# One tile buffer goes from V's gather ring to U's in a mixer and expert-lookup layer

## What is computed

```python
q = (xt @ w_query).reshape(T, Hh, 2, PEER_HALF)              # 8 heads
s = jnp.einsum('thpc,pnc->thpn', q, sub_keys)
sv, si = lax.top_k(s, K)                                     # K = 16
...
fv, fi = lax.top_k(cand, K)
eidx = jnp.take_along_axis(cidx, fi, axis=-1)                # 16 of 16384 experts per head
g = jax.nn.softmax(fv, axis=-1)
ue = expert_u[eidx]
ve = expert_v[eidx]
act = jax.nn.gelu(jnp.einsum('td,thkd->thk', xt, ue))
return jnp.einsum('thk,thkd->td', g * act, ve)
```

## Time and profile before

| | |
|---|---|
| median of three runs | 3078.46 us |
| profiled execution | 3075.11 us |
| its span, first to last instruction | 3073.6 us |
| TensorE busy (matmul) | 2595.0 us, 84% |
| VectorE busy | 2138.0 us, 70% |
| POOL busy | 1633.1 us, 53% |
| ScalarE busy | 804.2 us, 26% |
| bytes moved | 1071.89 MB, 349 GB/s over the span |
| of that by POOL's gathers | 805.40 MB |

### The profile page before, as it was taken

How to read it: one execution, slowest core, us unless ns; L and a number is a source line. 1 busy time by engine, 2 the same in 40 slices (tenths; PEclk the granted TensorE clock), 3 DMA queues, 4 the chain that set the end, 5 groups by cost and what they waited for, 6 DMA issues and landing times.

```text
span 3073.6 us, 38707 instructions
## 1 busy us (share of the span) xinstructions
PE 2595.0 (84%) x13398; PEld 1675.4 (55%) x13398; DVE 2138.0 (70%) x5237; ACT 804.2 (26%) x1798; POOL 1633.1 (53%) x1565
## 2 busy tenths in 40 slices
PE   8999998766867768688777686667999999999998
PEld 6898544334444434454444452445666666666664
DVE  5451666569899788888898786773677755555556
ACT  2231113113223233232342333881111101000001
POOL 0000477677666656666656566673544554555554
PEclk9999999878878889898888797788999999999999
DMA  7103799999999999999999899999999999999998
GB/s 263 49 29 141 259 371 382 388 399 367 398 392 361 401 346 379 394 349 359 381 360 365 315 368 380 372 384 399 372 359 367 378 403 401 397 401 401 403 402 316
DMA packets 340953, 1071.89 MB, mean 349 GB/s; under 512 B 33876, under 2 KB 74136, under 8 KB 339736
## 3 DMA queue, kind: packets, MB, share of 16 engines
q0 software_dynamic: 221184, 805.40, 67.7%
q1 hardware_dynamic: 119576, 264.01, 23.1%
HBM read 1029.03 MB, written 40.26 MB: 348 GB/s over the span
## 4 chain that ended last, share of the span: by engine, by line
PE 58%; DVE 14%; DMA 12%; ACT 5%; issue 5%; POOL 4%; SPq 1%; DVEq 0%; ACTq 0%; POOLq 0%
PE bank L2220 21%; PE xs_ahead L2220 16%; PE xs L2220 15%; PE acc L2220 6%; DMA weights<-u_blocks 5%; DVE work L2032 5%; DMA work<-expert_u,chosen 4%; POOL work L1259 2%; POOL work L1279 2%; DVE work L1682 2%; DVE work L1690 2%; ACT work L1299 1%; ACT work L1464 1%; DVE rest L1916 1%; ACT work L1463 1%
## 5 line engine op out<-in xcount | busy, mean ns | idle before, releaser
L1259 POOL DMA_INDIRECT work<-expert_u,chosen x716 | 777.6, 1086 | 818.6 <-DVE dots L2032 322.1
L1279 POOL DMA_INDIRECT work<-expert_v,idx_v x516 | 524.1, 1016 | 366.4 <-PE acc L2220 226.7
L2032 DVE CUSTOM_DVE_ANT_0 work<-work,xs 128x1024 f32<-128x1024 f32 x418 | 506.3, 1216 | 62.0 <-DMA work<-expert_u,chosen 51.2
L2220 PE MATMUL bank<-weights 128*128 128x256 f32 x2016 | 461.4, 382 | 17.2 <-DMA weights<-u_blocks 17.2
L2220 PE MATMUL xs_ahead<-work 64*128 64x128 f32 (+3 forms) x1746 | 395.2, 392 | 69.2 <-ACT weights L1299 41.9
L2032 DVE CUSTOM_DVE_ANT_0 work<-work 128x1024 f32<-128x1024 f32 x298 | 364.2, 1223 | 127.1 <-DMA work<-expert_u,chosen 123.7
L2220 PEld LDWEIGHTS bank<-weights 128*128 128x128 f32 x2016 | 384.7, 192 | 121.4 <-issue 51.9
L2220 PE MATMUL acc<-work,lw 128*32 128x512 f32 x2064 | 335.8, 715 | 80.7 <-DMA work<-expert_v,idx_v 79.2
L2220 PEld LDWEIGHTS xs_ahead<-work 128*128 128x128 f32 (+1 forms) x1746 | 232.0, 205 | 219.5 <-issue 186.4
L1682 DVE TENSOR_TENSOR work<-work,weights 128x256 f32<-128x256 f32 x128 | 54.5, 426 | 374.0 <-ACT work L1552 294.0
L2220 PEld LDWEIGHTS bank<-n2T,weights 128*128 128x128 f32 x2048 | 263.4, 210 | 56.3 <-issue 55.6
(11 more groups left out here) (278 smaller groups left out, 3530.5 us busy)
## 6 DMA issues: line engine op xcount, KB each, us to landing
work<-expert_v SPq DMA_DIRECT2D x128, 512.0 KB, 15.0
weights<-u_blocks SPq DMA_DIRECT2D x126, 512.0 KB, 16.2
work<-kv_dram SPq DMA_DIRECT2D x72, 256.0 KB, 6.8
weights<-w_dram SPq DMA_DIRECT2D x32, 512.0 KB, 22.3
w_dram<-weights SPq DMA_DIRECT2D x7, 2048.0 KB, 10.8
weights<-w_in SPq DMA_DIRECT2D x6, 2048.0 KB, 19.2
work<-expert_u,chosen POOLq DMA_INDIRECT x716, 8.4
mix_dram<-work SPq DMA_DIRECT2D x34, 256.0 KB, 5.1
```

Of the source, the lines that this page charges most:

```text
L1259: pool.indirect_dma_start(out=slot(s), out_offset=None, in_=expert_u, in_offset=bass.IndirectOffsetOnAxis(ap=chosen[:, G % PICKED_HEADS, k ...
L1279: pool.indirect_dma_start(out=slot(s), out_offset=None, in_=expert_v, in_offset=bass.IndirectOffsetOnAxis(ap=picks, axis=0)).then_inc(v_la ...
L2032: nc.vector.tensor_tensor_reduce(slot(s), slot(s), rows, 1.0, 0.0, ALU.mult, ALU.add, dots[:, d:d + 1]).then_inc(dotted, 1)
L2220: return nc.tensor.matmul(out_, lhsT, rhs, start=start, stop=stop, skip_group_check=True)
```

## The change

Buffer 4 leaves V's ring, which took it over together with buffer 5 at gather 20, and joins U's ring at gather 38. V's ring has seven buffers from gather 20 on (eight before), eight from 92 (nine) and sixteen from 624 (seventeen). U's ring has five from gather 38 (four), six from 56 (five), seven from 76 (six) and eleven from 640 (ten). The landings of V are counted in four groups where there were five.

```diff
-V_SETS = 5
+V_SETS = 4
...
-V_RINGS = [(0, [8, 9, 10, 11, 14, 15, 29, 30]), (ARENA_V, [14, 15, 4, 5, 8, 9, 10, 11]),
-           (92, [28, 14, 15, 4, 5, 8, 9, 10, 11]),
-           (624, [16, 17, 18, 19, 20, 21, 22, 23, 28, 4, 5, 8, 9, 10, 11, 14, 15])]
-U_RINGS = [(0, [0, 1, 2, 3]), (56, [6, 0, 1, 2, 3]), (76, [7, 6, 0, 1, 2, 3]), (640, [24, 25, 26, 27, 7, 6, 0, 1, 2, 3])]
+V_RINGS = [(0, [8, 9, 10, 11, 14, 15, 29, 30]), (ARENA_V, [14, 15, 5, 8, 9, 10, 11]), (92, [28, 14, 15, 5, 8, 9, 10, 11]),
+           (624, [16, 17, 18, 19, 20, 21, 22, 23, 28, 5, 8, 9, 10, 11, 14, 15])]
+U_RINGS = [(0, [0, 1, 2, 3]), (38, [4, 0, 1, 2, 3]), (56, [6, 4, 0, 1, 2, 3]), (76, [7, 6, 4, 0, 1, 2, 3]),
+           (640, [24, 25, 26, 27, 7, 6, 4, 0, 1, 2, 3])]
```

## The result

The change makes the kernel slower: 3129.84 us (median of four runs, 3114.57 to 3132.77) against 3078.34, ratio 1.0152 with a 95% interval of 1.0134 to 1.0171. A second measurement of the same kernel gave 3122.74 us, 1.0144 (1.0125 to 1.0162). The forecast was 3097; the direction was right, the loss is more than twice what the sum had.

The account below looks back on a forecast made before the run. POOL's waits for TensorE's sums, through V's tight ring, were taken to bound the middle. Terms 13.5 + 5.2 = 18.7 us on the profiled 3075.11 give 3093.8; adding 3.35 for the median gives 3097 us, range 3066 to 3122.

Parts of the forecast that it names:

- What bounds the kernel: In the middle, POOL waits 208.3 us for TensorE's sums and 42.0 for VectorE's dots: V's ring tight, U's nearly loose.
- The middle's term: V gathers 94 to 623, ring of nine to eight: each of five full stretches starts one pair late, 13.5 us.
- the five stretches: Parts of the middle between 780 and 1916 us where transfers are full, 376 to 411 GB/s; priced at 2.7 us each.
- the loose one of 411 us: Stretch of 1467 to 1878 us, transfers at 356 GB/s, share 0.93; the later U was to cost nothing while rows last.
- The ring of seven and the switch: V gathers 20 to 92 and the switch at 92: two waits for sums, partly covered by queued transfers, 5.2 us.
- the gather at 595 us: V gather of 595.60 would wait 9.2 us for a sum; 7.0 us of queue covers part, leaving 2.2 us.
- The dense stage: From 2120 to 2500 us, TensorE busy throughout; rings of 11 and 16 hold as many rows as 10 and 17: 0.
- The signs that were named: In the middle: dot waits near 0, sum waits near 208 us or more, VectorE's U waits up about 13; a POOL stand near 655.
- The hole of 1850: Between 1850 and 1854 us transfers run dry while POOL waits for a sum; claimed to last some 2.7 us longer.
- The queue hides it: Rival: in the middle, queued transfers (3.1 us) cover the 2.7 us shift; about 3078 us, chance 0.25.
- U's ring as the tight one: Rival: V's shorter ring costs nothing, U's longer ring helps the full stretches and before 690 us; 13 us faster, 3065, chance 0.16.
- The feedback rival: Rival: late V rows delay TensorE's sums, which hold V's next gathers and so U; 44 us, 3122 us, chance 0.10.

Follow-up runs that it names:

- V short alone: Against the kernel before: V's rings shortened as in the change, U's rings left as before; 3120.41 us, ratio 1.0134.
- V longer: Kernel before with buffers moved from U to V from gather 92: V ten, U five, 3062.44 and 3058.19 us; V eleven, U four, 3074.96 us.
- V later: Changed kernel's rings, each V gather issued one U gather later in POOL's order from U's gather 112 on; 3097.0 us, again 3098.11.
- V short early: Against the kernel before: V's ring has seven buffers from gather 20 to 91 only, U's rings as before; 3093.96 us, ratio 1.0048.
- the reverse run: Against the kernel before: buffer 7 goes from U to V from gather 92, V ten and U five; 3062.44 us, again 3058.19.

## Why the prediction was wrong

*What bounds the kernel: right.* V's ring was the tight one, POOL's order carries the wait to U, and U's extra buffer is worth nothing that these runs can tell. The runs with V short alone, with V longer and with V later show it, each from another side.

*The middle's term, 13.5 us: mis-sized, 26.5 to 33.1.* The step that failed is "Between the full stretches the engines have rows in hand, and the later U costs nothing as long as those last". It priced what lies between the five stretches at nothing, and that cost 19.7 of the 33.1 us. Dot 433 lies in the middle of the loose one of 411 us. The rows in hand were not looked up gather by gather: wherever a U row landed less ahead of its dot than it now comes late, VectorE stands, in a full stretch or not. "Everything behind is one pair, 2.7 us, later" was right for most gathers (2.4 us in the median), but a gather directly behind V's wait is late by the pair and the stand. The 13.5 us for the five full stretches come close to the 13.4 of the first trace, in part by luck: the sum took 2.7 us for each, and they lost between -1.4 and 6.5. That the ten groups above come to 2.7 us each bears out no price either, since they were picked for losing 2.0 or more.

*The ring of seven and the switch, 5.2 us: mis-sized, 14.1 and 14.3 in the two traces of the change, +16.0 us of time for the early part alone.* Here two steps failed, and a third agrees by luck. The lines, first of the kernel before, then of the change:

```profile
436.30 0.94 POOL L1279 DMA_INDIRECT work<-expert_v,idx_v  x1 [4.91 <-PE xs L2220]
...
605.05 0.94 POOL L1279 DMA_INDIRECT work<-expert_v,idx_v  x1 [6.39 <-PE acc L2220]
```
```profile
428.61 0.94 POOL L1259 DMA_INDIRECT work<-expert_u,chosen  x1 [0.30 <-issue]
437.45 0.94 POOL L1279 DMA_INDIRECT work<-expert_v,idx_v  x1 [7.90 <-PE xs L2220]
...
609.33 0.94 POOL L1279 DMA_INDIRECT work<-expert_v,idx_v  x1 [7.05 <-PE acc L2220]
...
671.75 1.82 POOL L1279 DMA_INDIRECT work<-expert_v,idx_v  x1 [5.71 <-PE acc L2220]
```

At the switch the queue of transfers was to cover 4.7 of the 7.7 us. POOL stood 5.71 us at V's gather 93, where it hadn't stood before, and the trace falls from 8.6 to 14.1 us behind there: 5.5 us against 3.0, so the queue covered next to nothing. V's first use of buffer 5 one gather earlier was counted as nothing, "at worst a pair of 2.7 us". The stand for the projection was there before, at V's gather 23; it now comes at gather 22, one pair earlier, and VectorE is 3.6 us behind at dot 48. For the gather at 595 us the sum has 2.2 us, and 2.4 are lost between dots 92 and 96; but the reading behind it, 9.2 us of new standing less 7.0 of queue, was wrong. The kernel before stands for that same sum already, 6.39 us at the next gather of V (605.05, gather 76), which the sum overlooked; the change stands at gather 75. So this stand, too, only came one pair earlier, some 2.5 us.

*The dense stage, 0: off.* Every run with V's ring short in some part loses 3 to 10 us from dot 560 on, in the change 6.1 of its 10.4 by dot 576, where the dense stage begins. V short early loses 4.1 there, though its rings from gather 92 on are those of the kernel before, so smaller rings in the dense stage can't be the whole cause. No run took this part alone; the cause stays open.

*The signs that were named.* POOL's waits for dots went to 11.6 us, its waits for sums grew from 236.3 to 274.2 us (both targets), and POOL stands near 655 us for a sum, at V's gather 93. The hole of 1850 is there, but at that place it is not 2.7 us longer. VectorE's waits for U grew by 38.7 us, not by about 13: the sign had the right direction and three times the size.

*The rivals.* "The queue hides it" fell: the trace has the delay in VectorE's waits. U's ring as the tight one fell with the reverse run. The feedback rival came closest in time, 3122 us, by luck: with V later still, TensorE waits longer for V (74.3 us) and the middle loses next to nothing. So V's late rows, on which its upper bound of 5.4 us a stretch was built, aren't the cause.

## What to carry to other kernels

Where one queue issues for two consumers, a wait in it is paid by the other consumer's transfers behind it: before a buffer is moved between rings, work out how late each of them will be (here a pair for most, a pair and the stand for the one directly behind), and compare that with its lead (from landing to use), place by place, not with the mean or with the transfer rate of the stretch. And look whether the kernel already stands for the same event one gather later: then the stand only moves. Give the buffer to the ring whose wait holds the queue, even if the other consumer is the one that is seen waiting. And the order of issue, or the order in which a ring starts on its buffers, can be worth as much as a buffer.
